# mLSTM steps that signal the output sums ahead of the state products, keys weighted on GpSimd, and a rearranged first norm and attention projection in a three-block transformer kernel

## The reference, cut to what matters

```
mod_x = split(silu(c) @ ada_w[layer] + ada_b[layer])           # shifts and scales, 6 x 1024 for x, the same for ctx
hx = rms_norm(x, norm1_g[layer]) * (1 + mod_x[1]) + mod_x[0]   # the norm "0a" for layer 0, "1a" for layer 1

# mLSTM, per head and direction (forward, backward), over blocks of tokens
s   = (q @ k^T) * d                  # d: decays, masked
num = s @ v + a * (q @ C)            # C: state carried from block to block
den = sum(s) + a * (q @ n)
h   = num / max(|den|, exp(-m))
C   = a * C + (k * w)^T @ v          # n the same with v = 1
h   = rms_norm(h_fwd + h_bwd) * sigmoid(o)

# attention of layer 1
q = rope(rms_norm(q, q_g)); k = rope(rms_norm(k, k_g))   # 16 query heads, 4 key heads, 64 wide
o = softmax(q k^T / 8) v
```

## Time and profile before

| | |
|---|---|
| median of 3 runs | 2734.12 us (2724.08 to 2736.72) |
| the profiled execution, its own time | 2727.04 us |
| its span, first to last instruction | 2725.3 us |
| PE busy | 2449.7 us (90%), mean granted clock 0.945 |
| DVE busy | 1515.5 us (56%) |
| ACT / POOL busy | 953.8 us (35%) / 1121.6 us (41%) |

### The profile page before, as it was taken

The page is one execution under the profiler, slowest core; times in us unless marked ns, Lnnn a source line. Parts: engine busy times, 40 slices in busy tenths (PEclk is TensorE's granted clock), DMA queues, the critical chain, the costliest instruction groups (busy, mean ns, idle before and its releaser), DMA issues.

```text
span 2725.3 us, 31892 instructions
## 1 busy us (share of the span) xinstructions
PE 2449.7 (90%) x11622; PEld 1979.2 (73%) x11622; DVE 1515.5 (56%) x2033; ACT 953.8 (35%) x1491; POOL 1121.6 (41%) x843
## 2 busy tenths in 40 slices
PE   6999769899999997769989999898798888899999
PEld 5888657788888886546668888676544565688887
DVE  6756756755555543988651222369578534452533
ACT  3312221512121224547652332353343343432322
POOL 1433003344444431347634557345454231344444
PEclk6999879899999998979989999899899899999999
DMA  5323103233333331231123332232300120232323
GB/s 226 116 95 130 47 1 121 88 103 113 109 107 115 103 114 39 82 71 41 45 72 100 100 92 92 77 101 79 114 1 0 44 73 16 84 95 92 100 93 108
DMA packets 68823, 231.69 MB, mean 85 GB/s; under 512 B 8049, under 2 KB 10993, under 8 KB 68593
## 3 DMA queue, kind: packets, MB, share of 16 engines
q1 hardware_dynamic: 68720, 230.35, 26.4%
HBM read 219.57 MB, written 2.10 MB: 81 GB/s over the span
## 4 chain that ended last, share of the span: by engine, by line
PE 72%; DVE 13%; issue 7%; POOL 4%; ACT 3%; DMA 0%; SPq 0%; POOLq 0%; DVEq 0%; ACTq 0%
PE PS L649 51%; PE PS L667 9%; POOL HL L519 4%; PE PS L686 2%; DVE RD L2276 2%; PE PS L618 1%; PE PS L1086 1%; PE PS L910 1%; DVE SM L2260 1%; PE PS L1179 1%; PE PS L1075 1%; DVE STATE L2115 1%; PE PS L792 0%; PE PS L795 0%; DMA EARLY<-adastream 0%
## 5 line engine op out<-in xcount | busy, mean ns | idle before, releaser
L519 POOL TENSOR_TENSOR HL<-RAW,HL 128x512 fp32r<-128x512 f32 x614 | 900.9, 1489 | 1454.7 <-ACT HL L1224 1454.5
L649 PE MATMUL PS<-HA,HL 128*128 128x512 f32 (+1 forms) x2592 | 555.9, 367 | 17.4 <-DVE V L2041 5.1
L649 PE MATMUL PS<-HID,HL 128*128 128x512 f32 (+1 forms) x2832 | 561.8, 360 | 0.0
L649 PE MATMUL PS<-HB,HL 128*128 128x512 f32 (+1 forms) x2592 | 540.0, 360 | 0.0
L649 PEld LDWEIGHTS PS<-HID,HL 128*128 128x128 f32 x2832 | 478.3, 188 | 81.9
L649 PEld LDWEIGHTS PS<-HA,HL 128*128 128x128 f32 x2592 | 445.5, 191 | 108.1 <-issue 31.5
L1224 ACT ACTIVATE HL<-RAW 128x1024 fp32r<-128x1024 f32 x307 | 323.2, 1053 | 498.7 <-PE PS L649 381.2
L649 PEld LDWEIGHTS PS<-HB,HL 128*128 128x128 f32 x2592 | 442.5, 189 | 75.0
L1893 DVE CUSTOM_DVE_ANT_0 ADJ<-ADA,CB 128x1024 f32<-128x1024 f32 x160 | 265.3, 1658 | 8.4 <-DVE X L1815 2.7
L1815 DVE SCALAR_TENSOR_TENSOR X<-PS,MOD,X 128x256 f32<-128x256 f32 (+1 forms) x120 | 75.8, 659 | 330.3 <-PE PS L649 312.2
L667 PE MATMUL PS<-HA,HL 128*128 128x256 f32 (+1 forms) x576 | 137.5, 402 | 61.5 <-DVE HA L1796 49.2
(11 more groups left out here) (372 smaller groups left out, 2744.7 us busy)
## 6 DMA issues: line engine op xcount, KB each, us to landing
RAW<-wstream SPq DMA_DIRECT2D x307, 512.0 KB, 3.5
ADA<-adastream SPq DMA_DIRECT2D x80, 512.0 KB, 3.7
EARLY<-adastream SPq DMA_DIRECT2D x16, 512.0 KB, 14.2
QB<-QH SPq DMA_DIRECT2D x32, 128.0 KB, 2.3
X<-x_in SPq DMA_DIRECT2D x8, 384.0 KB, 6.5
QC<-QL SPq DMA_DIRECT2D x16, 128.0 KB, 2.3
out<-X SPq DMA_DIRECT2D x8, 256.0 KB, 2.2
X<-mem SPq DMA_DIRECT2D x1, 1024.0 KB, 13.3
```

The source lines that it names most:

```text
L519: a = pool.tensor_tensor(HL[:, t % RING, 1, half], RAW[:, t % RAW_RING, half], HL[:, t % RING, 0, half].bitcast(F32), ALU.subtract)
L649: mm = pe.matmul(bank(t % 2, r), w[:, wp, k * P:(k + 1) * P], a[:, ap, lo:hi], start=(k == 0 and (wp, ap) == (0, 0)), stop=(k == nk - 1 an ...
```

## The change

Three places are edited; a fourth edit only merges semaphores of the MLPs (`hid_ready0`, 1, 2 into one, with offsets) and issues the same instructions.

1. First norm: PE takes 9 chunks and DVE 7; the groups waited for are now the first four loaded, the next four, and so on; PE sums the squares after two chunks; the root and the first two scalings stand on DVE after two of its seven chunks; ACT's root stands ahead of `high(0)` and `high(1)`, and `high(2)` stands inside the norm, ahead of chunk 3.
2. mLSTM: as the title says; DVE's inverses (and the second half) stand ahead of the state's update.
3. Attention projection: the root's square is taken by ACT (into R2), the squares and roots lie in the ctx part of X, the values' high part and the fixed constants are made by ACT, and the values' low part comes first on DVE. SP issues the 20 key moves ahead of the weight tiles `T_OUT1 + 2` to `T_OUT1 + 4`, and the load of `mem` after the query moves.

```diff
-ADA_PE = 8
+ADA_PE = 9
+        def early_group(j):
+            return min((j if j < ADA_PE else j - ADA_PE) // 2, 3)
...
@@ SP
-            stretch(t, T_OUT1 + RING + 1)
-            sp.wait_ge(S("norm_scaled"), of_norm("1a", "scaled", KC))
-            load(X[:, :, 0:NCTX], mem, "mem_in")
+            stretch(t, T_OUT1 + 2)
...                 (the 20 moves of the keys)
+            stretch(T_OUT1 + 2, T_OUT1 + RING + 1)
             sp.wait_ge(S("k_in"), 16 * 5 * KV_HEADS)
...                 (the moves of the queries)
+            load(X[:, :, 0:NCTX], mem, "mem_in")
@@ POOL
+            lows(0, 25 + AHEAD)
+            pool.wait_ge(S("act_once"), ACT_ONCE["cols_read"])
+            pool.wait_ge(S("tile_done"), 25)
+            for n in range(N_ML):
+                if WITH_STATE[n]:
+                    if n >= 2:
+                        pool.wait_ge(S("state_sums"), states_until(n - 1))
+                    pool.tensor_tensor(KW[:, n % 2, :, :], KTOK[:, b, :, :], EK..., ALU.mult).then_inc(S("k_weighted"), 1)
@@ PE
             for i in range(ADA_PE):
                 ada(i)
-            norm_sum("0a", "cx")
+                if i == 1:
+                    norm_sum("0a", "cx")
...
                     if n:
                         pe.wait_ge(S("num_read"), n)
-                        pe.wait_ge(S("state_new"), states_until(n))
+                    if n >= 2:
+                        pe.wait_ge(S("state_new"), states_until(n - 1))
...
+                    mm.then_inc(S("summed"), 1)
+                    if WITH_STATE[n]:
+                        pe.wait_ge(S("k_weighted"), states_until(n + 1))
+                        if n:
+                            pe.wait_ge(S("state_new"), states_until(n))
+                        (the two products of the state)
+                        mm.then_inc(S("state_sums"), 1)
@@ ACT
-            for t in range(AHEAD):
+            norm_root("0a", "cx")
+            for t in range(2):
                 high(t)
-            norm("0a", "cx", shift((0, 0)))
+            act.wait_ge(S("dve_once"), ONCE["first_gains"])
+            norm("0a", "cx", shift((0, 0)), root=False, between=lambda: high(2))
...                 (head_rsqrt)
+                act.activation(spans(R2[:, j % 2, 0:hi - lo]), r, ACT.Square).then_inc(S("hn_rsqrt"), 1)
+            def values_high():        # two copies of 1536 elements, after the first key tile
+            def fixed():              # waits k_in; IDR, QC, and six copies of 512, after the last root
@@ DVE
             for i in range(ADA_PE, ADA_FIRST):
                 ada(i)
+                if i == ADA_PE + 1:
+                    norm_root("0a", "cx")
...
-                if WITH_STATE[n]:
-                    dve.tensor_tensor(KW[:, n % 2, :, :], KTOK[:, b, :, :], EK..., ALU.mult)
...
-                    state(s - 1)
                     inverse(s - 1)
                     if SECOND[s - 1]:
                         second_half(s - 1)
+                    state(s - 1)
...                 (head_scale)
-                newton([(HR[:, j % 2, 0:n], PS[:, 5 + 2 * (j % 2), 0:n], HT[:, 0, 0:n])], HEAD_DIM)
+                link(dve.scalar_tensor_tensor(t2, spans(PS[...]), HEAD_DIM * EPS, t2, ALU.add, ALU.mult))
+                link(dve.scalar_tensor_tensor(r, t2, 3.0 * HEAD_DIM, r, ALU.subtract, ALU.mult))
```

More of the change, by code:

```diff
@@ L438, in _ @@
             for i in range(ADA_PE):
-                for j in (i, ADA_PE + i):
-                    load(early(j), adastream[j], f"early_in{j // 4}")
+                for j in (i, ADA_PE + i)[:1 + (ADA_PE + i < ADA_FIRST)]:
+                    load(early(j), adastream[j], f"early_in{early_group(j)}")
             for t in range(RING):
@@ L1248, in rsqrt, with norm_root @@
                 a.then_inc(S(sem), 1)
-            def norm(n, regions, bias):
+            def norm_root(n, regions):
                 act.wait_ge(S("norm_sum"), of_norm(n, "sum", 1))
@@ L1259, in norm @@
                 act.activation(RS[:, lo:hi], RS[:, lo:hi], ACT.Exp, scale=-0.5).then_inc(S("norm_rsqrt"), 1)
+            def norm(n, regions, bias, root=True, between=None):
+                if root:
+                    norm_root(n, regions)
                 for k in range(KC):
+                    if k == 3 and between:
+                        between()
                     act.wait_ge(S("norm_scaled"), of_norm(n, "scaled", k + 1))
@@ L1484, in _ @@
                         head_rsqrt(j)
+                if i == 1:
+                    values_high()
+                if i == SLOTS:
+                    fixed()
                 for j, job in enumerate(HJOBS):
@@ L1785, in acc_square, with scaled, norm_root @@
                 a.then_inc(S("norm_acc"), 1)
-            def norm(n, regions):
+            def scaled(n, k, lo, hi):
+                refined(T1[:, k % 2, lo:hi], X[:, k, lo:hi], RS[:, lo:hi], D).then_inc(S("norm_scaled"), 1)
+            def norm_root(n, regions):
                 lo, hi = span(regions)
@@ L1792, in norm @@
                          T2[:, 0, REG[r][0]:REG[r][1]]) for r in regions], D)
+                for k in range(2):
+                    scaled(n, k, lo, hi)
+            def norm(n, regions, root=True):
+                lo, hi = span(regions)
+                if root:
+                    norm_root(n, regions)
                 def low(k):
@@ L1970, in _ @@
                 ada(i)
+                if i == ADA_PE + 1:
+                    norm_root("0a", "cx")
+            modulation(0, ADA_PE, ADA_FIRST)
             modulation(0, 0, ADA_PE)
-            modulation(0, ADA_PE, ADA_FIRST)
             gains(0, 1, PC["n1g"])
-            norm("0a", "cx")
+            dve.sem_inc(S("dve_once"), 1)
+            norm("0a", "cx", root=False)
             dve.memset(V1[:, :, :, ML_DV:ML_DV + 1], 1.0)
@@ L2109, in state @@
                 d, b = ML_STEPS[n]
-                dve.wait_ge(S("summed"), n + 1)
                 if WITH_STATE[n]:
+                    dve.wait_ge(S("state_sums"), states_until(n + 1))
                     for c in range(2):
@@ L2121, in inverse @@
                 den, lim, e = numerators()[:, :, :, ML_DV], two(EMC[:, b, d, :]), two(DEN[:, n % 2, :])
+                dve.wait_ge(S("summed"), n + 1)
                 if n >= 2 and not SECOND[n - 2]:
```

119 lines of the change are left out of this document (66 added, 53 removed).

## The result

The changed kernel takes 2693.35 us (median of four runs, 2689.14 to 2698.59) where the kernel before takes 2729.1 beside it: a ratio of 0.9875, 95% interval 0.985 to 0.990, or 34 us by the ratio. The forecast was 2712.6 us (0.992) with a range of 2697 to 2727. The profiled execution of the changed kernel took 2689.14 us, 37.9 less than the profiled one of before.

What follows compares the result with a forecast made beforehand. The prediction took PE's matrix work to bound most of the span, with gains only where PE waits: 3.5 (first norm) + 13.5 (mLSTM) + 4.5 (attention projection) = 21.5 us, from 2734.1 to 2712.6 us, range 2697 to 2727.

Steps and rivals of the forecast that it cites:

- Bound and places: Whole kernel: mostly PE's matrix work, so gains come only where PE waits: first norm, mLSTM, attention projection.
- Rival C: Later stages: what is gained is given back by half or more, 2724 us; chance 0.07.
- signs of being wrong: PE's clock falling in plain steps, PE's ninth chunk ending after 53, or ACT's fixed constants ending after DVE's last rotation.
- Given back: First norm: lost from the 5.9 us gain, 1.05 us to `high(2)` in ACT's queue and 1.3 us to POOL contention.
- I take off 2 us for the clock: mLSTM: 2 us deducted from 15.5 because some of the stage will again run at 1.2 GHz, leaving 13.5 us.
- the steps up to 4: mLSTM: a 5 us DVE reciprocal ahead of `inverse(1)`, then second halves and normalization filling DVE; gain 4.1 us.
- 4 x 1.8 = 7.2 us: mLSTM, steps 4 to 8: four plain intervals each go from 6.2 to 4.4 us, with PE their bound.
- From 8 to 11: mLSTM: DVE carries about 7 us a step and the state's update only moves behind; gain 4.2 us.
- Rival B: mLSTM stays a loop of latencies at the low clock, giving 4 instead of 13.5; total 2722 us; chance 0.15.
- the bounds of 0.75 to 1.5: mLSTM: a KW product on POOL costs at most 0.75 to 1.5 us and is hidden unless over 8 us.
- Rival A: Attention projection: the tile's load isn't held by the key moves, adding 9 us of gain, 2704 us; chance 0.13.
- Rival D: Attention projection: slower by the new wait on SP; 35 us of moves for no change, 48 for slower; chance 0.03.

Runs made afterwards that it cites:

- after_again: The changed kernel run once more, nothing edited, beside three other kernels; ratio 0.9875 (0.9847 to 0.9904) to the kernel before.
- kw_on_dve: Changed kernel with the mLSTM's keys weighted by DVE again, ahead of the mask, instead of GpSimd; ratio 0.9876 (0.9847 to 0.9905).
- load_first: Changed kernel with the load of weight tile T_OUT1 + 2 issued ahead of the 20 key moves; ratios 0.9857 and 0.9855, medians 2692.63 and 2690.22 us.

## Why the prediction was right in direction and too small

**Bound and places: right.** The gain came at the three places named. With the mean over all kernels of each kind: first norm 6.1 us (82.0 to 75.9), mLSTM 18.9 (102.3 to 83.4), heads' stage 8.1 (92.9 to 84.8), in all 33.1 of the 34 measured. Rival C fell, with nothing given back later: from the mLSTM's out projection to the first head's sum it is 685.9 us before and 685.3 after, and from the attention's start to the end 1546.8 and 1545.3. None of the prediction's signs of being wrong came up either; all of them would have meant a smaller gain. What failed is the size of the terms, that of the mLSTM most.

**First norm: the steps were right, "Given back" was mis-sized.** The prediction had the first projection at 57 us; it is at 55.5 in the mean, and at 56.4 in the executions whose first two chunks ran nearly all at the low clock. `high(2)` and the contention were put at 2.35 us; 20.4 us for the pair of tiles against 19.1 says 1.3, of which `high(2)` alone is 1.05, so little is left for the contention. Prediction 3.5 us (bounds 1 to 4.9), measured 5.3 in those executions, 6.1 in the mean and 8.2 in the luckiest. The bound didn't allow for the second level of the clock: I took a chunk at 3.43 us for all nine, though the earlier trace rows had no chunk ahead of 22.87, and in the 4.9 us before that the granted clock was still 0.95. That the first profile lay so far out was luck.

**mLSTM: the term "I take off 2 us for the clock" has the wrong sign, and the steps up to 4 were mis-sized.** The loop opened as described: plain steps were predicted at 4.4 us and took 4.44 to 4.63, with PE busy all the time. For the intervals from 4 to 8 I took 4 x 1.8 = 7.2 us from one step of before (first row), and this was wrong twice. The first of the four isn't plain: PE waits there for the normalization of a block. The other three weren't all at the full clock before. The four intervals of before:

```profile
331.63:338.89 7.26, 4.98 (x39) 4.46 (x37) 4.36 (x14) 2.35 (x8) 0.00 (x0) 1.00 0.00 0
338.89:346.71 7.82, 6.19 (x34) 5.26 (x33) 4.43 (x12) 1.77 (x7) 0.00 (x0) 0.78 0.00 0
346.71:354.56 7.85, 6.21 (x33) 5.35 (x33) 4.51 (x13) 2.15 (x7) 0.00 (x0) 0.79 0.01 2
354.56:360.78 6.22, 4.59 (x33) 4.06 (x33) 3.24 (x10) 1.62 (x6) 0.00 (x0) 1.00 0.00 1
```

And of the changed kernel, the first one and then the other three together:

```profile
314.81:323.40 8.59, 6.64 (x39) 5.79 (x38) 4.26 (x13) 1.72 (x6) 0.61 (x1) 0.80 0.00 0
323.40:336.98 13.58, 13.57 (x98) 12.06 (x96) 10.48 (x30) 6.13 (x18) 1.84 (x3) 1.00 0.01 1
```

The first takes 6.92 us where the clock is full (`after_again`), so at the full clock on both sides the change is worth 0.3 us there and about 1.65 in each of the others, 5.3 in all: less than 7.2. But the mean gain of the four intervals is 9.3 us, so some 4 us of it are the clock, by this estimate. Over these steps the three profiles with the old order had 0.77 to 0.88, and the seven with all of this part had 0.92 or 1.00. The prediction took 2 us off for the clock where it gave some. Why the clock stays up isn't shown. In the three steps without a gap on PE it was 1.00, but the last step of before had 1.00 too, with gaps, and no run changed the gaps alone.

In the steps up to 4 the mean gain was 6.4 us, not 4.1. KW off DVE, which I had mentioned ("matters only where DVE is full") and not counted, can be about 1.2 of it (`kw_on_dve`). Here too the clock differs, and the rest stays open. From 8 to 11 it was 3.1 (4.2 predicted), in the tail 0. In all that is 18.8 against 13.5, just over my upper bound of 18. Rival B fell.

**KW on GpSimd: hidden, as predicted, and shorter.** The eight products inside the loop took 0.61 us each, below the bounds of 0.75 to 1.5. PE never waited for them, and DVE kept its usual times: `STATE` 1.44 us beside the product, as in the earlier trace rows. Four of the eight start with the update, which reads PSUM, and beside the other four DVE runs instructions that read PSUM or have one input. So the rule that GpSimd and a VectorE instruction with two SBUF inputs exclude each other (the Trainium skill, SBUF — State Buffer, "SBUF: two separate sides") cost nothing in these eight, not the 5 us that it could have. Of the two products ahead of `sums(0)`, one took 0.61 us and the other 1.6, beside an `ADJ` of DVE (two SBUF inputs) that took 1.52 instead of 1.23. There the trace agrees with the rule, and so it does in the attention projection, where a low part on GpSimd and such an instruction met: `QA<-QA,X` took 1.66 us beside a low part at 1099.03, and 0.69 alone at 1112.55.

**Attention projection: right in every link, 3.6 us too small.** Four low parts of keys are ready 46.8 us after the first head's sum (51.0 before, so 4.2 sooner, not 3.1); the tile lands 16.8 us after the first move, not 18; and from there to the attention it is 21.0 us, not 22. Each is off by about one microsecond, all to the same side; against the mean of the eight kernels that is 8.1 us, not 4.5. Rival A, the load not held by the moves, is not what the change does; `load_first`, where the load stands ahead of them, gives 7.5 us more (I had 9). Rival D, slower by the wait on SP, fell: it would have needed 35 us of moves, and they took 12.8.

**The range.** Its lower end, 2697, stood on the sum of central values and one rival at a time. Three terms that each erred by caution add up: 2.6, 5.4 and 3.6 us. The first two had a deduction (contention, clock) that was larger than any row bore out, and the range treated errors as if they would cancel.

## What to carry to other kernels

When a loop of several engines is cut below one engine's own work, read every step of the old loop, not one: some aren't plain, and some ran at the low clock. Price each against what it really took, and don't deduct for the clock without a row that says so; here the shorter loop ran at a higher clock, not a lower one. An early signal is worth only what its reader does first with it; look at the reader's order before the signal. When small transfers are moved ahead of a big one in one queue, ask who reads the big one and what stands behind that reader; here one load placed ahead of twenty moves was worth 7.5 us.

## What the runs showed of the hardware that was not expected

Between executions of the same code the clock falls at different moments, and this is a part of the spread of the runs. The two chunks at 19 us took 4.06 to 6.89 us. The stretch from the out projection behind the attention to the end took 1383.0 to 1385.2 us in eight profiles and 1390.0 to 1395.1 in six, with no value between. It isn't the kernel: the changed kernel had 1383.8 and 1391.0 in its two profiles, `load_first` 1395.1 and 1385.2. In the two that I compared, most of the loss is in one stretch of 100 us, in which DVE is busy for 76 to 84 us and PE has gaps. Windows at the same distance from the attention's start, of the changed kernel first:

```profile
1994.00:2094.00 100.00, 88.60 (x281) 46.06 (x280) 84.34 (x171) 42.08 (x72) 37.12 (x26) 0.95 0.00 1
```

Then `load_first`:

```profile
1990.00:2090.00 100.00, 83.73 (x256) 44.19 (x256) 75.61 (x163) 38.46 (x65) 38.19 (x27) 0.88 0.00 0
```

What decides between the two wasn't found; no run was made for it.
